# Second expert pass of a hybrid decoder step: the gathered rows are weighted and summed on VectorE, tokens on the partitions, in place of one-column TensorE products

## The reference, cut to what matters

```python
# per token t, over its 128 picked experts e with softmax gate g[t, e]
dot[t, e] = h[t] . peer_u[e]               # h: the normed residual, 1024 long
y[t] += g[t, e] * gelu(dot[t, e]) * peer_v[e]   # peer_v[e]: a row of 1024
```

## Time and profile before

| | before |
|---|---|
| time, median of 3 runs | 2902.37 us (2901.86 to 2903.58) |
| profiled execution, span | 2903.8 us |
| busy PE / DVE / ACT / POOL | 2569.2 / 1443.5 / 1030.4 / 896.8 us |
| expert stage, from the first gather to the last copy of its result | 1840.5 to 2790.2 us |
| DMA moved by the whole program | 511.22 MB |

### The profile page before, as it was taken

How to read it: one execution, slowest core, us unless ns; L and a number is a source line. 1 busy time by engine, 2 the same in 40 slices (tenths; PEclk the granted TensorE clock), 3 DMA queues, 4 the chain that set the end, 5 groups by cost and what they waited for, 6 DMA issues and landing times. The chain is left out here.

```text
span 2903.8 us, 51463 instructions
## 1 busy us (share of the span) xinstructions
PE 2569.2 (88%) x20574; PEld 2165.9 (75%) x20574; DVE 1443.5 (50%) x3149; ACT 1030.4 (35%) x1819; POOL 896.8 (31%) x782
## 2 busy tenths in 40 slices
PE   7984887898866998799999988799999999999969
PEld 6973885686545978799999877667777777677748
DVE  3354444314744224479999855344444444444443
ACT  2012111223622020134444466444444444444432
POOL 0000000000000000001111555577777777777710
PEclk9986997897976999899999999899999999999989
DMA  3210000522212220156656444899999999999932
GB/s 118 81 34 21 4 4 18 184 83 69 64 35 66 66 88 30 58 176 186 184 183 186 144 173 173 294 344 349 337 336 344 345 350 337 335 346 358 342 129 69
DMA packets 206886, 511.22 MB, mean 176 GB/s; under 512 B 31938, under 2 KB 99010, under 8 KB 205186
## 3 DMA queue, kind: packets, MB, share of 16 engines
q1 hardware_dynamic: 150338, 340.04, 34.8%
q0 software_dynamic: 56320, 167.98, 16.0%
HBM read 463.49 MB, written 48.56 MB: 176 GB/s over the span
## 5 line engine op out<-in xcount | busy, mean ns | idle before, releaser
L2335 POOL TENSOR_TENSOR wide<-wide,sif 128x2048 f32<-128x2048 f32 (+1 forms) x10 | 52.7, 5267 | 1580.8 <-DVE wide L2451 1580.8
L2585 POOL DMA_INDIRECT dots<-dots,place x320 | 373.7, 1168 | 125.8 <-issue 97.2
L2589 POOL DMA_INDIRECT v_row<-in_peer_v,expert x320 | 367.0, 1147 | 97.5 <-issue 97.5
L2720 DVE TENSOR_TENSOR v_lo<-v_raw,v_hi 128x1024 fp32r<-128x1024 f32 x128 | 157.1, 1227 | 367.9 <-ACT v_hi L2669 367.9
L2200 PE MATMUL ps<-h_hi,u_hi 128*128 128x320 f32 x1024 | 321.5, 314 | 10.7 <-DVE u_lo L2357 10.7
L2200 PE MATMUL ps<-h_lo,u_hi 128*128 128x320 f32 x1024 | 317.5, 310 | 0.0
L2200 PE MATMUL ps<-h_hi,u_lo 128*128 128x320 f32 x1024 | 317.4, 310 | 0.0
L2611 PE MATMUL ps<-h_hi,u_hi 128*128 128x256 f32 x1024 | 300.6, 294 | 11.5 <-DVE u_lo L2715 11.5
L2611 PE MATMUL ps<-h_lo,u_hi 128*128 128x256 f32 x1024 | 292.4, 286 | 0.0
L2611 PE MATMUL ps<-h_hi,u_lo 128*128 128x256 f32 x1024 | 292.2, 285 | 0.0
L2611 PEld LDWEIGHTS ps<-h_hi,u_hi 128*128 128x128 f32 x1024 | 197.8, 193 | 87.0 <-issue 70.2
(11 more groups left out here) (489 smaller groups left out, 5257.9 us busy)
## 6 DMA issues: line engine op xcount, KB each, us to landing
u_raw<-in_peer_u SPq DMA_DIRECT2D x256, 512.0 KB
v_raw<-in_peer_v SPq DMA_DIRECT2D x128, 512.0 KB
dots<-dots SPq DMA_DIRECT2D x128, 160.0 KB, 1.8
g<-gate_matrix SPq DMA_DIRECT2D x32, 512.0 KB, 8.0
wt<-in_w_in SPq DMA_DIRECT2D x24, 512.0 KB, 3.6
pages<-in_cmp_pages SPq DMA_DIRECT2D x64, 128.0 KB, 2.0
kv_pages<-in_sel_pages SPq DMA_DIRECT2D x64, 128.0 KB, 2.0
wt<-in_w_zg SPq DMA_DIRECT2D x16, 512.0 KB, 3.6
```

The lines of the kernel that those rows point to most:

```text
L2335: nc.gpsimd.tensor_tensor(hot4, hot4, which, ALU.mult).then_inc(numbered, 1)
L2585: nc.gpsimd.indirect_dma_start(dots[:, s:s + 1], None, dots_flat, bass.IndirectOffsetOnAxis(f.place[:, s:s + 1], 0)).then_inc(d_got[s % SL ...
L2589: nc.gpsimd.indirect_dma_start(v_row(s), None, v_rows, bass.IndirectOffsetOnAxis(f.expert[:, s:s + 1], 0)).then_inc(v_got[s % SLOTS], 16)
L2720: nc.vector.tensor_tensor(v_lo[:, j % 2], v_raw[:, j % RV], v_hi[:, j % 2].bitcast(F32), ALU.subtract).then_inc(v_parted, 1)
```

## The change

The sparse tokens are now gathered the other way round: a row tile holds on each *partition* one token, and one tile is one of the token's 128 experts. Three groups of tokens (two of 128, and the last 64 twice, the even experts on the lower 64 partitions, the odd ones on the upper) make ROW = 5 tiles for every two experts, 64 batches, NR = 320 tiles: as many gathers as before. DVE multiplies each tile by the per-partition weight and adds it to one of three sums `f.y` in SBUF (`mix_row`, one `scalar_tensor_tensor` of 128 x 1024 each). The PE products, the copies out of PSUM, the stores to DRAM and the read back in `collect_stage` go. The rows, the dots and the addresses are laid out by DVE in `search_stage` at the end of `finish(n)` for the last three tiles of tokens (`address_rows`), without the transposes; the scores of the last 64 tokens are made on both halves of the partitions (16 more PE products). POOL issues the dots of a batch two batches ahead (AHEAD), then five rows one after the other.

```diff
-BT = 4
-NB = TX // BT
+ROW = 5
+NB = N_KEYS // 2
+NR = NB * ROW
...
+                if n >= TD // P:
+                    dve.wait_ge(chosen, n + 1)
+                    address_rows(n - TD // P)
+
+            def address_rows(m):
+                ch.link(nc.vector.scalar_tensor_tensor(out=number[:], in0=num[:, 0, :], scalar=float(N_KEYS), in1=num[:, 1, :],
+                                                       op0=ALU.mult, op1=ALU.add))
...
+                for rows, to, of in wanted:
+                    numbers = by_pair(number)[rows, :, of]
+                    nc.vector.tensor_copy(by_batch(f.expert)[rows, :, to], numbers)
+                    nc.vector.tensor_scalar(by_batch(f.place)[rows, :, to], numbers, float(TX), own_t[rows, m:m + 1],
+                                            ALU.mult, ALU.add)
+                    last = nc.vector.tensor_copy(by_batch(f.gate)[rows, :, to], by_pair(num[:, 2, :])[rows, :, of])
...
+    AHEAD, RD = 2, 6
+    last_step = NT
+    rows_at = {j: [ROW * ((j - 1) // 2) + i for i in ((0, 1, 2) if j % 2 else (3, 4))] for j in range(1, NT + 1)}
+    gates_at = {j: j // 2 for j in range(0, NT, 2)}
+    which = (0, 1, 2, 0, 1)
...
-            for s in range(SLOTS):
-                fetch_dots(s)
-                fetch_rows(s)
-            for b in range(NB - SLOTS // BT):
-
-                pool.wait_ge(summed, 2 * b + 2)
-                for i in range(BT):
-                    fetch_dots(b * BT + SLOTS + i)
-                    fetch_rows(b * BT + SLOTS + i)
+            for b in range(AHEAD):
+                fetch_dots(b)
+            for b in range(NB):
+                if b + AHEAD < NB:
+                    fetch_dots(b + AHEAD)
+                for i in range(ROW):
+                    fetch_row(ROW * b + i)
...
-            def mix_rows(j, half):
-                for b in mixing.get(j, ()):
...
-                        mm = nc.tensor.matmul(k.ps[32 * i:32 * i + 1, 6 + half, :], dots[:, s:s + 1],
-                                              v_row(s)[:, half * 512:half * 512 + 512], start=True, stop=True)
...
+            def mix_row(s):
+                b, i = s // ROW, s % ROW
+                y = f.y[:, which[i], :]
+                if i == 0:
+                    dve.wait_ge(sgated, b + 1)
+                dve.wait_ge(v_got[s % SLOTS], 16 * (s // SLOTS + 1))
+                if s >= 2:
+
+                    dve.wait_ge(mixed, s - 1)
+                nc.vector.scalar_tensor_tensor(out=y, in0=v_row(s), scalar=dots[:, s:s + 1], in1=y, op0=ALU.mult,
+                                               op1=ALU.add).then_inc(mixed, 1)
...
             for j in range(-2, last_step + 1):
+                own = rows_at.get(j, [])
                 if 0 <= j < NT:
                     weigh(j)
                 if 0 <= j + 2 < NT:
                     part_u(j + 2)
                 if 0 <= j < NT:
                     part_w(j)
+                if j == 1:
+                    dve.wait_ge(cleared, 1)
+                for s in own[:1]:
+                    mix_row(s)
                 if 0 <= j + 1 < NT:
                     part_v(j + 1)
-                gate_rows(j)
+                for s in own[1:]:
+                    mix_row(s)
+                if j in gates_at:
+                    gate_rows(gates_at[j])
```

More of the change, by code:

```diff
@@ L2154, in search_stage @@
         slots = k.sb(ctx, "slots", [P, N_KEYS])
-        number = k.sb(ctx, "number", [P, TX])
-        place = k.sb(ctx, "place", [P, TX])
+        number = k.sb(ctx, "number", [P, N_KEYS])
+        own_t = k.sb(ctx, "own_t", [P, 4])
         stored = k.sems(ctx, *[f"stored{e}" for e in range(RD)])
@@ L2211, in scores @@
                         half = slice(c * HD, c * HD + HD)
-                        mm = nc.tensor.matmul(k.ps[0:rows, 2 + 2 * c + hd // 4, (hd % 4) * N_KEYS:(hd % 4 + 1) * N_KEYS],
-                                              q[half, hd, at:at + rows], keys[half, hd, :], start=True, stop=True)
+                        for part in parts:
+                            mm = nc.tensor.matmul(k.ps[part, 2 + 2 * c + hd // 4, (hd % 4) * N_KEYS:(hd % 4 + 1) * N_KEYS],
+                                                  q[half, hd, at:at + part.stop - part.start], keys[half, hd, :], start=True,
+                                                  stop=True)
                 mm.then_inc(scored, 1)
@@ L2240, in spread_gates @@
                 mm.then_inc(spread, 1)
[L2242 removed]
+            pe.wait_ge(loaded, 64)
             scores(0)
@@ L2482, in _ @@
                 step()
[L2483 to L2494, removed]
 def experts_stage(k, h, f, us):
@@ L2532, in experts_stage @@
         w_lo = k.sb(ctx, "w_lo", [P, 2, TD], F32R)
-        dots = k.sb(ctx, "dots", [P, TX])
-        rows = k.sb(ctx, "rows", [P, 2, D_MODEL])
+        dots = k.sb(ctx, "dots", [P, NR])
         slots = k.sb(ctx, "v_row", [P, SLOTS, D_MODEL])
@@ L2561, in _ @@
                 load_g(i)
-            for j in range(last_step + 3):
+            for j in range(NT):
                 if j + RU < NT:
@@ L2683, in gelu, with gelu_dots @@
                 nc.scalar.activation(act_t[:, j % 2], up_bank(j), ACT.Gelu_apprx_tanh).then_inc(gelued, 1)
[L2685 to L2695 removed]
+            def gelu_dots(b):
+                act.wait_ge(d_got[b % RD], 16 * ROW * (b // RD + 1))
+                own = dots[:, b * ROW:(b + 1) * ROW]
+                nc.scalar.activation(own, own, ACT.Gelu_apprx_tanh).then_inc(sgelued, 1)
+            for j in range(-2, NT):
+                if j + 2 < NT:
                     round_u(j + 2)
[L2697 removed]
+                if j >= 0:
                     round_w(j)
[L2699 to L2705 removed]
+                if j in gates_at:
+                    gelu_dots(gates_at[j])
                 if 0 <= j + 1 < NT:
```

135 lines of the change are left out of this document (52 added, 83 removed).

## The result

The changed kernel takes 2918.8 us (median of 5 runs, 2914.64 to 2930.46), the kernel before beside it 2903.58 us (5 runs, 2901.86 to 2905.8): ratio 1.0053, 95% interval 1.0035 to 1.0071. It is slower, but by 15 us where 90 were forecast, outside the range. The profiled execution spans 2920.2 us against 2903.8.

What follows compares the result with a forecast made beforehand. POOL, issuing 640 gathers without a break, was taken to bound the expert stage. Gather holds +95, ends -3, collect_stage -6, search_stage +4 gave +90 on 2903.8 - 1.4: 2992 us, range 2935 to 3060, eight times in ten.

Steps and rivals of the forecast that it cites:

- POOL's gathers bound the stage: Expert stage: POOL issues 640 gathers without a break, 935 us with no slack; PE has some 28 us of slack.
- `mix_row` holds gathers: Expert stage: mix_row, reading two SBUF operands, holds up POOL's gathers as the subtractions do; the forecast itself, chance 0.78.
- Rival B: Expert stage: mix_row does not hold POOL, 640 gathers still take 935 us; 2897 us, chance 0.08.
- I take two thirds of the upper end, some +95, p = 1.61: Expert stage: price of mix_row holding POOL, between 0 and +135 (+146 against measured 935); p is time per gather in us.
- the check against 1.48: Expert stage before the change: the independent-phase rule gave 1.48 us per gather, measured 1.46, so it was said to hold.
- that escape: Expert stage: a freed gather returns 1.25 us later, past a back-to-back instruction (1.14 us), so some gathers escape; reason for two thirds.
- PE's gain is worth nothing: Expert stage: PE loses 166 us of busy time, 908 to 742, worth nothing as long as POOL needs 935.
- Ends -3: Ends of the expert stage: some 11 us behind the last gather against 14 now, so -3 us.
- collect_stage -6: collect_stage: PE's wait for rows read back goes, but for the start of the stage, -6 us.
- search_stage +4: search_stage: extra PE products and small DVE instructions cost +4 us in all, 0 to 8.
- Expected signs: Trace signs: gathers' mean about 1300 ns, minimum 940, ending 0.81 us behind mix_row; last starts some 1030 us after first.
- Rival D: Expert stage: DVE and POOL brake one another at a quarter of the gathers, +204 us, 3101 us, chance 0.09.

Runs made afterwards that it cites:

- mix_psum: Changed kernel with mix_row adding all rows into one sum in PSUM instead of three in SBUF (sums mixed): 2890.65 us, ratio to the kernel before 0.9947.
- mix8: Changed kernel with mix_row working on only 8 of the 1024 columns of each row tile: 2863.86 us, ratio to the kernel before 0.9868.
- mix_last: Changed kernel with v_lo ahead of all mix_row of its step on DVE: 2881.63 us, ratio to the kernel before 0.9925.
- mix_halves: Changed kernel with every mix_row in two instructions of 512 columns: 2996.49 us, ratio to the kernel before 1.0311.
- spacer: Changed kernel with an unused tensor_reduce of 256 columns on DVE behind every mix_row: 2942.42 us, ratio to the kernel before 1.013.
- before_few: Kernel before with one gather of dots for each batch of four tokens in place of four: 2879.1 us, ratio to the kernel before 0.9922.
- after_few: Changed kernel with one gather of dots for each batch of five row tiles in place of five: 2765.31 us, ratio to the kernel before 0.9521.
- mix_mid: Changed kernel with v_lo behind all mix_row of its step on DVE: 2940.57 us, ratio to the kernel before 1.013.
- psum0: Changed kernel with the first of the three sums in PSUM, everything computed: 2920.36 us, ratio to the kernel before 1.0043.
- last_psum0: Changed kernel with v_lo ahead of all mix_row and the first of three sums in PSUM, everything computed: 2879.09 us, ratio to the kernel before 0.9924.
- last_subhalves: Changed kernel with v_lo ahead of all mix_row and u_lo and v_lo each in two half-width instructions: 2883.78 us, ratio to the kernel before 0.9944.

## Why the prediction was wrong, step by step

- **POOL's gathers bound the stage: shown.** POOL waits for practically nothing but "issue" in both kernels; halves of the subtractions make the kernel before 27 us faster, and `v_lo` first the changed one 37 us, with no work taken away while the stretch from the first gather to the end of the last shrinks by 38 and 39 us. With fewer gathers both fall too, the changed one by 153 us.
- **`mix_row` holds gathers: shown**, by the row at 2138.28 and by `mix_psum`, where it does not. Rival B is out, though its 2897 was nearer to the measured time (22 us off) than my 2992 (73 us).
- **The step that failed is the price of the hold: "I take two thirds of the upper end, some +95, p = 1.61".** Measured: p = 963.1 / 640 = 1.505, +27.6 us. The wait per long instruction did not stay near the 0.53 of before, it fell to 163 / 576 = 0.28. The "two thirds" came from no row; the upper end rested on phases that are independent, by which a gather is held as often as DVE is busy. Before, that is 410 / 936 of the 640, 281, and 221 are held: near enough for the check against 1.48 to come out, with DVE idle more than half of the stage. After, it is 769 / 964 of them, 510, and only 315 are held, for 0.52 us instead of 0.60. So the check said nothing for a DVE that is four fifths busy. There the phases are not independent: 159 of the 315 wait 0.2 to 0.3 us. A freed gather comes back 1.25 us later, beside a spacing of 1.14 and 1.20 us on DVE. 193 gathers of the change come right after a held one with a long instruction standing directly behind the one that held it: 110 get through, 33 wait for a part of an instruction, 50 for all of it. In the kernel before there is no such place. Which of these happens hangs on the order: 124, 163 and 190 us for three orders of the same instructions, 244 for `mix_row` in halves. My reasoning named that escape but not that it could be most of the cost, in either direction; a reckoning by lengths alone did not give this term. The range should have reached from below 0 (`mix8` and `mix_last` have less wait than the kernel before) to beyond +100.
- **PE's gain is worth nothing: right.** PE busy 788 us in the stage, I said 742; its first `down` products take 452 ns in the mean against 413. Of the 502 of them in the stage, 95 take over 0.56 us, and 90 of these 95 start while the granted clock is at the lower of its two levels (1.2 GHz), against 7 of the other 407.
- **`mix_row` 1.27 us: 1.289.** DVE is not the bound: right, it idles 189 us ahead of `mix_row`.
- **Ends -3: +4.5**, five `mix_row` were still queued on DVE. **collect_stage -6: -8.3. search_stage +4: -2.5.** Another -4.9 us arise ahead of the first `u` product, which the forecast left out.
- **Expected signs:** minimum of 940 ns, 0.82 us behind the end of a `mix_row`, the idle time ahead of it, and ACT's wait for dots (2.4 us left of 277) as forecast; the mean of 1300 ns was not (1201), nor the 1030 us from the first to the last gather (962).
- Rival D (the two brake one another at a quarter of the gathers) did not come in the change, where 63 of 640 gathers wait longer than 1 us. `mix_halves` shows something near to it, at +78 us, by gathers that are passed over at a boundary and not, as D had it, by meeting the next instruction but one.

What stays open: why a gather at the start of a `mix_row` gets through and one at the start of a `v_lo` does not. The traces narrow it down. I counted them over nine runs (both kernels, `spacer`, `before_few`, `after_few`, `mix_last`, `mix_mid`, `psum0`, `last_psum0`), at the long instructions with all operands in SBUF. A gather that starts 0.06 to 0.08 us after the start of a `mix_row` gets through in 98 of 108 cases, whatever stands ahead of it; so late after the start of a subtraction, in none of 32. Within 0.02 us of the start it gets through at a `mix_row` in 247 of 247 cases, at a subtraction in 9 of 9 if DVE was idle ahead of it, but in 18 of 170 if a `mix_row` stands right ahead. So both the instruction and its neighbour count. Which property of theirs does it (operands, data types, waits), none of the runs separates, nor why a gather is passed over at a boundary.

## What to carry to other kernels

Look whether the engine that issues indirect DMAs ever waits for anything; if it issues without a break through the whole stage, its issues are the bound, though its busy share (79% here) is below that of another engine, and work taken from other engines gives nothing by itself. Where VectorE instructions with two SBUF operands run beside such issues, their lengths gave no price here once VectorE was four fifths busy: try their order and their splitting on the chip, which here was worth 59 us between the best and the worst order. Before moving work to an engine with idle time, ask which issues that idle time lets through.

## What the runs showed of the hardware that was not expected

A gather held by DVE is not always freed at the end of the instruction that it met: in `mix_halves` 143 gathers were held over one or more boundaries, up to three, in `spacer` 88, in the change 38, in the kernel before none. A gather that just gets through can make the `mix_row` longer, by more the later it comes: over five runs (the change, `spacer`, `mix_last`, `mix_mid`, `last_subhalves`), 183 `mix_row` beside a gather that started up to 0.02 us after them took 1.28 us, as do those with no gather near, and 82 beside one that started 0.06 to 0.08 us after them took 1.33 us. And the large MEMSET ahead of the stage did not lengthen the first gather (1.16 us, as without it), but the second took 3.01 us beside it and the `u_lo` behind it, the longest of the 640.
